# Dividing the latent attention's last half head inside the differential attention

## The reference

```python
def mla_attention(...):                 # six latent heads
    sc = q_nope @ k_nope.T + q_rope @ k_rope.T
    p = softmax(sc * scale)
    return p @ v

def diff_attention(...):                # four differential heads, two maps each
    p = softmax(q[m] @ k[m].T * scale + bias)      # m = 0, 1
    a = p[0] - lam * p[1]
    return rms_norm(a @ v) * (1 - lam_init)
```

## Time and profile before

| | before |
|---|---|
| median of 3 runs | 3967.64 us (3961.53 to 3970.51) |
| profiled execution, time | 3965.12 us |
| its span | 3963.3 us |
| mean granted clock of TensorE | 0.984 |
| TensorE matmuls busy | 3778.7 us, 95% |
| VectorE busy | 2181.7 us, 55% |
| ScalarE busy | 1742.3 us, 44% |
| GpSimd busy | 2296.7 us, 58% |

### The profile page before, as it was taken

One profiled execution on the slowest core, in us unless ns is written; L12 is line 12 of the kernel. 1 busy time (PEld: TensorE's weight loads), 2 busy tenths in 40 slices (PEclk: granted clock), 3 DMA queues, 4 the chain that ended last, 5 costly groups with the idle time before them and its releaser, 6 DMA issues. The chain is left out here.

```text
span 3963.3 us, 52431 instructions
## 1 busy us (share of the span) xinstructions
PE 3778.7 (95%) x19002; PEld 2633.9 (66%) x19002; DVE 2181.7 (55%) x3987; ACT 1742.3 (44%) x3136; POOL 2296.7 (58%) x1381
## 2 busy tenths in 40 slices
PE   8999999999999999989989999999999899998899
PEld 8789775555546666657877897755555466665577
DVE  3003024665559999875531030245555599997755
ACT  3102102433339999861031021023333499997610
POOL 1231324877768999744512213257777699996455
PEclk9999999999999999999999999999999999999999
DMA  5434445223312222245454344432224102223353
GB/s 176 124 128 131 134 145 131 66 56 87 82 41 47 58 58 59 56 114 195 149 162 128 128 130 138 141 77 59 56 56 108 40 22 58 58 59 85 107 176 135
DMA packets 181063, 392.50 MB, mean 99 GB/s; under 512 B 18206, under 2 KB 100360, under 8 KB 169160
## 3 DMA queue, kind: packets, MB, share of 16 engines
q1 hardware_dynamic: 179944, 387.75, 35.2%
q10 hardware_dynamic: 864, 1.41, 0.2%
HBM read 255.94 MB, written 135.67 MB: 99 GB/s over the span
## 5 line engine op out<-in xcount | busy, mean ns | idle before, releaser
L1336 POOL TENSOR_TENSOR mla_sum_pool<-mla_sum_pool,mla_probs 128x1024 f32<-128x1024 f32 (+1 forms) x336 | 778.1, 2316 | 207.6 <-ACT mla_probs L1297 182.8
L1354 DVE TENSOR_REDUCE carry_row_max<-psum 128x1 f32<-128x512 f32 x688 | 474.8, 690 | 412.9 <-PE psum L1162 408.6
L1297 ACT ACTIVATE mla_probs<-psum 128x1024 f32<-128x1024 f32 x384 | 373.5, 1021 | 694.3 <-PE psum L1199 687.1
L1749 POOL TENSOR_TENSOR diff_probs<-diff_probs 128x1024 f32<-128x1024 f32 x252 | 598.8, 2376 | 78.1 <-ACT diff_probs L1692 67.2
L1680 ACT ACTIVATE diff_probs<-psum,diff_shift 128x1024 f32<-128x1024 f32 x384 | 426.2, 1117 | 22.1 <-DVE diff_shift L1777 21.2
L656 PE MATMUL psum<-in_x_hi,in_w_hi 128*128 128x512 f32 x1024 | 410.0, 400 | 2.7 <-ACT in_mla_val L764 2.7
L656 PE MATMUL psum<-in_x_hi,in_w_lo 128*128 128x512 f32 x1024 | 405.8, 396 | 0.0
L656 PE MATMUL psum<-carry_firsts,in_w_hi 128*128 128x512 f32 x1024 | 404.7, 395 | 0.0
L1212 PE MATMUL psum<-mla_probs,mla_v_op 128*64 128x512 f32 x1536 | 373.2, 607 | 0.0
L1619 PE MATMUL psum<-ident,diff_probs 128*128 128x128 f32 x2048 | 319.7, 279 | 10.2 <-ACT diff_turned L1702 4.6
L1767 DVE TENSOR_REDUCE diff_part_shift<-psum 128x1 f32<-128x1024 f32 x256 | 311.2, 1217 | 25.5 <-PE psum L1460 17.3
(11 more groups left out here) (249 smaller groups left out, 7381.7 us busy)
## 6 DMA issues: line engine op xcount, KB each, us to landing
in_w_raw<-in_w_in SPq DMA_DIRECT2D x64, 512.0 KB, 3.8
split_d<-in_out SPq DMA_DIRECT2D x32, 512.0 KB, 2.7
split_d<-handed SPq DMA_DIRECT2D x32, 512.0 KB, 2.7
carry_firsts<-split_d SPq DMA_DIRECT2D x48, 256.0 KB, 8.0
carry_weights<-split_d SPq DMA_DIRECT2D x48, 256.0 KB, 8.0
carry_weights<-split_d SPq DMA_DIRECT2D x16, 768.0 KB, 18.4
carry_rows<-in_x SPq DMA_DIRECT2D x16, 512.0 KB, 3.7
raw_d<-in_out SPq DMA_DIRECT2D x16, 512.0 KB, 2.6
```

Source lines behind the costliest of these rows:

```text
L1297: nc.scalar.activation(probs[:, s % RING, :].rearrange("p (a n) -> p a n", n=CH), psum[:, S0 + 2 * (s % 2):S0 + 2 * (s % 2) + 2, :], ACT.E ...
L1336: nc.gpsimd.tensor_tensor(acc, start, probs[:, s % RING, mine], ALU.add).then_inc(pool_added, 1)
L1354: nc.vector.tensor_reduce(row_max[:, u % 2, qb, n:n + 1], psum[:, sweep_bank(g), :], AX.X, ALU.max).then_inc(maxed, 1)
L1749: nc.gpsimd.tensor_tensor(probs[:, n % DEEP, at], probs[:, n % DEEP, at], second, ALU.add).then_inc(mixed, 1)
```

## The change

The last unit of the latent attention is no longer divided in its own stage. ScalarE copies both inputs of the division, the raw output from PV and the total from AUX, into the two halves of `o_out`, after the stores that still read these halves. In the differential attention VectorE divides them there in eight pieces of 64 columns, one behind the copy in each of units 6 to 13; the product overwrites the raw half. SP's two stores of the result move behind the loads of head 1 and wait for the eighth piece. Three semaphores are new.

```diff
+                    if u < LAST:
+                        nc.scalar.activation(o_raw[:, u % 2, :], psum[:, PV, :], ACT.Copy).then_inc(pv_copied, 1)
+                        return
+                    act.wait_ge(o_stored[1], 32 * (LAST // 2))
+                    nc.scalar.activation(o_out[:, 1, :], psum[:, PV, :], ACT.Copy).then_inc(pv_copied, 1)
+                    act.wait_ge(o_stored[0], 32 * (UNITS // 2))
+                    act.wait_ge(z_psum, UNITS)
+                    nc.scalar.activation(o_out[:, 0, :], psum[:, AUX, :], ACT.Copy).then_inc(last_out, 1)
...
-                def divide_last():
-                    dve.wait_ge(z_psum, UNITS)
-                    dve.wait_ge(pv_copied, UNITS)
-                    dve.wait_ge(o_stored[LAST % 2], 32 * (LAST // 2))
-                    nc.vector.reciprocal(psum[:, AUX, :], psum[:, AUX, :]).then_inc(inverted, 1)
-                    dve.wait_ge(inverted, PIECES * LAST + 1)
-                    nc.vector.tensor_tensor(o_out[:, LAST % 2, :], o_raw[:, LAST % 2, :], psum[:, AUX, :], ALU.mult
-                                            ).then_inc(o_ready, PIECES)
...
+    PIECES, DIVIDE_AT = 8, 6
...
+                load(1)
                 last = o_d[(MLA_HEADS - 1) * DV:MLA_HEADS * DV, HALF:SEQ].rearrange("d (a n) -> a d n", n=CH)
+                sp.wait_ge(latent_divided, PIECES)
                 for a in range(2):
                     sp.dma_start(last[a], carry["o_out"][a * DV:(a + 1) * DV, 1, :]).then_inc(carry_sems["o_stored1"], 16)
-                load(1)
...
+                def divide_latent(piece):
+
+                    at = slice(piece * CH // PIECES, (piece + 1) * CH // PIECES)
+                    total, raw = carry["o_out"][:, 0, at], carry["o_out"][:, 1, at]
+                    nc.vector.reciprocal(total, total).then_inc(latent_inverted, 1)
+                    dve.wait_ge(latent_inverted, piece + 1)
+                    nc.vector.tensor_tensor(raw, raw, total, ALU.mult).then_inc(latent_divided, 1)
...
                     copy(n - LAG - 1, 3)
+                    if DIVIDE_AT <= n < DIVIDE_AT + PIECES:
+                        divide_latent(n - DIVIDE_AT)
```

More of the change, by code:

```diff
@@ L1042, in latent_attention @@
             sem(n) for n in ("scored", "exped", "pool_added", "pv_done", "pv_copied", "z_psum", "o_ready"))
-        inverted, dve_added, scored_ahead = sem("inverted"), sem("dve_added"), sem("scored_ahead")
+        inverted, dve_added, scored_ahead, last_out = (
+            sem(n) for n in ("inverted", "dve_added", "scored_ahead", "last_out"))
         if tables:
@@ L1281, in raw_out @@
                         act.wait_ge(o_ready, PIECES * (u - 1))
-                    nc.scalar.activation(o_raw[:, u % 2, :], psum[:, PV, :], ACT.Copy).then_inc(pv_copied, 1)
+                    if u < LAST:
[6 more added lines that the diff above has]
+                    nc.scalar.activation(o_out[:, 0, :], psum[:, AUX, :], ACT.Copy).then_inc(last_out, 1)
                 for s in range(STEPS + LAG + 1):
@@ L1409, in _ @@
                     elif kb == Z_AT + 1:
-                        if u == UNITS:
-                            divide_last()
-                        else:
+                        if u < UNITS:
                             for n in range(PIECES):
@@ L1511, in diff_attention @@
             sem(n) for n in ("times_ratio", "mixed", "turn_done", "pv_done", "odd_out", "o_ready"))
+        latent_inverted, latent_divided = sem("latent_inverted"), sem("latent_divided")
         dve_copied, act_copied, dve_mixed = sem("dve_copied"), sem("act_copied"), sem("dve_mixed")
```

## The result

The changed kernel takes 3973.02 us (median of 20 runs, 3968.19 to 3978.87) against 3966.61 before (20 runs beside them): +6.4 us, a ratio of 1.0017 with a 95% interval of 1.0011 to 1.0023, that is 4.4 to 9.1 us slower. The time lies in the stated range. The forecast of 3976.4 is 3.4 us too high: 1.0 us of it is the kernel before, whose median is 3966.61 over 20 runs and was 3967.64 over three, and 2.4 us is the change, +6.4 instead of +8.8. Whether the change exceeds the 0.2% bound, to which the prediction gave 0.50, the interval leaves open.

A forecast was written before the change was run, and what follows sets the result against it. No engine has room in units 6 to 13, and VectorE ends the seam last. Per layer 8 x 1.15 - 2.6 = 6.6 us added, 2.2 removed; +8.8 us for two layers, median 3976.4, range 3965 to 3984.

The forecast's parts named there:

- the 0.2% bound: Whole kernel: 7.9 us, about what a measurement can tell from no change; chance of slower 0.50, same 0.47, faster 0.03.
- The seam: Between latent and differential attention: removing the division gains 2.2 us a layer, because TensorE is late next.
- The hidden copy of ScalarE: At the end of the latent stage: one more 0.60 us copy out of PSUM, over 1.4 us before TensorE, costing nothing.
- SP's moved stores: On SP's queue: the last half head's two stores, behind head 1's loads and waiting for the eighth piece, cost nothing.
- The piece: VectorE, units 6 to 13: reciprocal plus a multiply held until GpSimd's instruction ends, 1.15 us each, bounds 0.72 and 1.47.
- Rival 1: Units 6 to 13: the multiply is not held up, 0.72 us a piece, +2 us in all, 3969.7; chance 0.22.
- What is hidden: Units 6 to 13: VectorE's own waits take in 2.6 us of eight pieces a layer, bounds 2.0 and 3.8.
- the wait before the copy: VectorE in units 6 to 13: a wait summing to 1.2 us, counted on to hide 0.2 us per two units.
- Units after 13 that run shorter than before: Differential attention from unit 14: a sign the prediction is wrong; it expected 7.22 us a unit as before.
- Rival 2: Differential attention: the stage takes the pieces in and only the seam's gain is left, -4.4 us, 3963.3; chance 0.09.
- Rival 3: Units 6 to 13: GpSimd's next instruction goes before the waiting multiply, 2.35 us a piece, +25.6 us, 3993; chance 0.06.
- Rival 4: Start of the differential attention: a shorter pause may shift TensorE's clock, 1.4 us a layer either way; no chance of its own.

The follow-up runs named there:

- seam_only: The changed kernel without any division piece, the last half head stored undivided and its store waiting for none: ratio 0.9988 against the kernel before.
- log_over_seam: The changed kernel dividing without VectorE: ScalarE takes the totals' logarithm in the latent stage and exp(-x) in the next, GpSimd multiplies there; ratio 0.9994 against before.
- reciprocal_only: The changed kernel with the multiply of each piece left out and the reciprocal kept, so the last half head is not divided: ratio 0.9992 against before.

## Why the prediction was right

**The seam**: right, 2.19 and 2.18 us against 2.18 and 2.19. The hidden copy of ScalarE: right. SP's moved stores: no cost appeared. In seam_only, where the stores wait for no piece, units 14 to 63 take 353.66 us, no less than the 353.34 of the change.

**The piece**: the mechanism was right, taken over from the 128x512 additions of the earlier trace rows to 64 columns: what is left of GpSimd's instruction + 0.08 (0.56 = 0.48 + 0.08 in unit 6). The price is 9.5 / 8 = 1.19 us against 1.15; the reciprocal takes 0.54 us, not 0.56. Rival 1 is out, and with it the reading of the earlier trace rows: in log_over_seam a product of 128x32 is held up as well when GpSimd streams 128x512; the free one stood beside a GpSimd instruction of two columns, and so it is in all 32 places of the kernel before where these two meet (0.191 to 0.195 us). By the rule of the Trainium skill (SBUF — State Buffer, section Who interferes with whom), named before as disagreeing with the trace in that one place, the sixteen multiplies and, in log_over_seam, the products of lambda must stand, and here the trace agrees: 0.49 to 1.03 us, and 0.93 for the pair.

**What is hidden**: mis-sized. I had 2.6 us of eight pieces, 3.4 were hidden (9.5 - 6.07). My account of where was wrong too. I let only 0.24 us through in an even unit, since ScalarE would be late for the rest, and counted on the wait before the copy. In the profile after the wait before the fourth maximum is used up whole, 1.9 us, and that before the copy stays. The parts are 1.9 + 0.7 for the output, 0.6 because maxima and outputs that no longer wait overlap with their neighbours (their busy time falls from 19.5 + 1.7 to 19.0 + 1.6 us), and 0.23 given back after unit 13: 0.35 us in units 14 to 21 (57.17 us instead of 57.52), of which 0.12 is lost again later. Units after 13 that run shorter than before were among the prediction's signs of being wrong; here they are worth 0.23 of 9.5 us. The same mis-sizing shows across the runs: the stage hides 3.3 of 3.7 us, 3.7 of 5.7, and 3.4 of 9.5, whether the 9.5 is made by two instructions a unit or by one. So at this place it takes in about 3.3 to 3.7 us of eight pieces whatever they cost, near my upper bound of 3.8, and what a layer pays beyond that is kept, as the prediction had it. The sum of a layer is then 9.5 - 3.4 - 2.2 = 3.9 us, 7.8 in two, where the forecast was 8.8 and the measurement 4.4 to 9.1. That 2.6 came within 0.8 us of the measured 3.4 is in part luck, since the waits that I had counted on were not the ones that were used.

**Rival 2** (the stage takes the pieces in) is right in a part that I had missed: a piece of 0.46 us is taken in nearly whole (reciprocal_only keeps 0.43 of 3.7 us). At the same place in the unit it was the size of the pieces that decided. **Rival 3** did not occur: GpSimd's next instruction follows without a pause, 7 to 31 ns ahead of the end that the profile gives the addition, and the multiply still ends 0.08 us after that end. **Rival 4**: the stretch to unit 4 is 25.89 and 26.22 us against 26.44 and 25.03, 0.6 us more over both layers. It is within the 1.4 us a layer that I allowed, but its cause is open: the 25.03 is the lowest of all profiled layers (see seam_only), and of the kernel before there is only the one profile.

## What to carry to other kernels

Moving an instruction changes where its operands lie, and that can cost more than its own time: a VectorE instruction with both inputs in SBUF that starts while GpSimd streams a tile ends only when that GpSimd instruction has ended (16 of 16 here), so place it where GpSimd waits, or leave one input in PSUM. A full stage has small waits in each unit, here 3.8 us over eight units, and work cut smaller than those waits goes in nearly free, while 5.2 us of work in one piece was kept whole and came with a lower clock of TensorE. At a seam count the gain only up to the engine that is late next.

## What was not expected of the hardware

A single VectorE delay of 5.2 us cost 6.7 and 7.7 us, with TensorE's granted clock at 0.76 to 0.95 in the two units around it. The table loads for a logarithm and an exponential, one after the other, were two, 1.28 us each; the Trainium skill (ScalarE: Activation LUTs, section Table sets: the hidden batching unit) says that one set holds both functions and one load does for both, and this compiled kernel did not get that.
